# Second attention of a four-layer kernel: index scores placed inside the first query group, eight projection steps ahead of the first scores, output weights' low parts allowed from the second keys on

## What is computed

```python
a_q, a_k, a_v, b_q, b_k, b_v, i_q, i_k, i_w = jnp.split(h @ w_in, EVEN_SPLITS, axis=-1)
...
o_a = diff_attention(a_q, a_k, a_v, lam, subln, lambda_init)
...
rel = jax.nn.relu(jnp.einsum('bqhd,bkd->bqhk', qiblk.astype(jnp.float32), kif))
score = jnp.einsum('bqhk,bqh->bqk', rel, wiblk.astype(jnp.float32))
score = jnp.where(mask[None], score, -jnp.inf)
_, idx = lax.top_k(score, topk)
...
return jnp.concatenate([o_a, o_b], axis=-1) @ w_out
```

## Time and profile before

| | |
|---|---|
| median of three executions | 1785.41 us |
| the profiled execution's own time | 1787.7 us |
| span of its trace | 1785.9 us |
| mean granted TensorE clock in it | 0.987 of full |
| busy: PE, DVE, ACT | 97%, 64%, 50% |
| the stretch around the change | 960 to 1090 us of the span |

### The profile page before, as it was taken

How to read it: one execution, slowest core, us unless ns; L and a number is a source line. 1 busy time by engine, 2 the same in 40 slices (tenths; PEclk the granted TensorE clock), 3 DMA queues, 4 the chain that set the end, 5 groups by cost and what they waited for, 6 DMA issues and landing times.

```text
span 1785.9 us, 22395 instructions
## 1 busy us (share of the span) xinstructions
PE 1735.7 (97%) x9104; PEld 1444.5 (81%) x9104; DVE 1141.9 (64%) x1588; ACT 897.9 (50%) x1282; POOL 7.7 (0%) x21
## 2 busy tenths in 40 slices
PE   8999999999999999999999989999999999999998
PEld 5898788888867888888888867888888889778887
DVE  3779978779666754565547967554655556675553
ACT  4645644465657444554444566444544445574432
POOL 0000000000000000000000000000000000000000
PEclk9999999999989999999999999999999999999999
DMA  9957677866615665555555324545554556345451
GB/s 385 379 227 295 238 306 294 305 244 230 258 72 189 235 222 179 200 191 181 176 201 183 119 71 177 183 171 188 204 186 175 192 205 224 111 149 181 170 195 47
DMA packets 54984, 363.45 MB, mean 204 GB/s; under 512 B 5841, under 2 KB 9041, under 8 KB 14690
## 3 DMA queue, kind: packets, MB, share of 16 engines
q1 hardware_dynamic: 53122, 351.47, 53.6%
q0 software_dynamic: 1760, 10.56, 1.5%
HBM read 360.96 MB, written 1.05 MB: 203 GB/s over the span
## 4 chain that ended last, share of the span: by engine, by line
PE 79%; DVE 10%; ACT 2%; issue 1%; DMA 0%; DVEq 0%; ACTq 0%
PE pp L633 76%; DVE low L1892 3%; PE pp L908 2%; DVE raw L1905 1%; PE pp L840 1%; DVE hf L2036 1%; PE pp L985 1%; ACT wh L1350 1%; DVE hl L1892 0%; DVE Sb L2187 0%; DVE sc L2288 0%; DVE x L1895 0%; DVE tb L1892 0%; DVE h L1892 0%; DVE top L2285 0%
## 5 line engine op out<-in xcount | busy, mean ns | idle before, releaser
L1892 DVE TENSOR_TENSOR low<-raw,wh 128x2048 fp32r<-128x2048 f32 (+3 forms) x346 | 638.8, 1861 | 367.9 <-ACT wh L1350 367.7
L1350 ACT ACTIVATE wh<-raw 128x2048 fp32r<-128x2048 f32 (+3 forms) x352 | 537.2, 1544 | 417.5 <-PE pp L633 288.1
L633 PE MATMUL pp<-wh,hh 128*128 128x512 f32 x1312 | 522.7, 398 | 7.4 <-ACT hh L1617 2.2
L633 PE MATMUL pp<-low,hh 128*128 128x512 f32 x1312 | 514.0, 392 | 1.8 <-DVE low L1892 1.6
L633 PE MATMUL pp<-wh,hl 128*128 128x512 f32 x1312 | 507.2, 392 | 3.7 <-DVE hl L1892 3.7
L633 PEld LDWEIGHTS pp<-wh,hh 128*128 128x128 f32 x1312 | 247.6, 189 | 65.3 <-issue 13.9
L633 PEld LDWEIGHTS pp<-wh,hl 128*128 128x128 f32 x1312 | 247.5, 189 | 57.6 <-DVE hl L1892 5.0
L633 PEld LDWEIGHTS pp<-low,hh 128*128 128x128 f32 x1312 | 248.0, 189 | 51.8 <-DVE low L1892 3.5
L633 PE MATMUL pp<-wh,hidh 128*128 128x512 f32 x592 | 232.0, 392 | 0.0
L633 PE MATMUL pp<-low,hidh 128*128 128x512 f32 x592 | 230.6, 389 | 0.3 <-DVE low L1892 0.3
L633 PE MATMUL pp<-wh,hidl 128*128 128x512 f32 x592 | 230.6, 389 | 0.0
(11 more groups left out here) (226 smaller groups left out, 1190.7 us busy)
## 6 DMA issues: line engine op xcount, KB each, us to landing
raw<-in_w SPq DMA_DIRECT2D x300, 1024.0 KB, 4.8
raw<-in_w SPq DMA_DIRECT2D x24, 768.0 KB, 4.3
raw<-in_w SPq DMA_DIRECT2D x13, 512.0 KB, 19.1
firstw<-in_w SPq DMA_DIRECT2D x6, 1024.0 KB, 14.8
gain<-in_w POOLq DMA_DIRECT2D x6, 512.0 KB, 4.8
bT<-in_rel POOLq DMA_DIRECT2D x1, 2048.0 KB, 12.0
cst<-in_csts POOLq DMA_DIRECT2D x1, 1029.0 KB, 7.2
xT<-in_xT SPq DMA_DIRECT2D x1, 1024.0 KB, 5.8
```

What stands on the lines that cost most here:

```text
L633: return e.matmul(out, lhsT, rhs, start=start, stop=stop, skip_group_check=True)
L1350: q.then_inc(e.activation(wh[j % NW][:, c], raw_of(i, kt * n)[:, c], ACT.Copy), s_wh, (j, part))
L1892: return e.tensor_tensor(out, a, b, op)
```

## The change

Three things are moved, all in the first layer of the second block.

1. The first block of index scores goes into the first query group, after six of its eight steps; the second block comes behind the group, and each later block stands one place earlier against the steps of `aqk` 1. On ACT the copy of `aqk` 0 for its rotation goes behind the relus of heads 0 to 3. DVE's order in this part stays as it is.
2. Eight fill steps in place of four run ahead of the attention pipeline, on all three engines, and `even_rate` gives two steps for six iterations in place of eight. The steps of attention a's norm (`oa_sums`, `oa_square`, `oa_root`, `oa_scale`) go two fill steps further down.
3. On DVE the limit that holds back the low parts of the output weights is lifted when the keys of b are done ("b"), no longer after b's values ("bv").

```diff
         def even_rate(i):
-            return 2 if i < 8 else 1
+            return 2 if i < 6 else 1
...
-                    if n == 2:
+                    if n == 4:
                         oa_sums(0)
...
-            whole("aqk", 0, h(7), (s_sq, (("rope", "aqk", 0),)), between=idx_rest)
-            q.wait_ge(s_side, ("rope", "idx", 0))
...
+            steps = group("aqk", 0, h(7), (s_sq, (("rope", "aqk", 0),)), between=idx_rest)
+            for _ in range(6):
+                next(steps)
             for n in range(2):
                 ixp.bufs[n], ixp.ends[n] = pairs.begin(("ix", n), (s_sideact, ("rl", 0, 5 + 2 * n)))
+            q.wait_ge(s_side, ("rope", "idx", 0))
+            index_scores(1, 0)
+            run(steps)
             steps = group("aqk", 1, h(7), (s_sq, (("rope", "aqk", 1),)))
-            for qb, jj, n in ((1, 0, 2), (1, 1, 2), (0, 0, 2), (0, 1, 2)):
+            for qb, jj in ((1, 1), (0, 0), (0, 1)):
                 index_scores(qb, jj)
-                for _ in range(n):
+                for _ in range(2):
                     next(steps)
-                if (qb, jj) == (1, 0):
+                if (qb, jj) == (1, 1):
                     rope(("rope", "aqk", 0), "64", 4, misc)
...
-            for n in range(4):
+            for n in range(8):
                 fill.step()
...
             ahead.group("aqk", 0)
-            rope_copy("aqk", 0, (s_side, ("rope", "aqk", 0)))
...
+                    if (qb, j) == (1, 4):
+                        rope_copy("aqk", 0, (s_side, ("rope", "aqk", 0)))
...
                 yield "b"
+                ahead.limit = of_group[("even_out", 0)][-1] + 1
...
-                ahead.limit = of_group[("even_out", 0)][-1] + 1
                 yield "bv"
```

More of the change, by code:

```diff
@@ L1690, in even_fill @@
                 for n, _ in enumerate(ahead.steps("bv", 0, "N")):
-                    if n == 1:
+                    if n == 2:
                         oa_square(0)
-                    if n == 2:
+                    if n == 4:
                         oa_root(0)
@@ L1860, in scalar_program @@
             fill = Fill(even_fill())
-            for _ in range(4):
+            for _ in range(8):
                 fill.step()
@@ L2327, in even_fill @@
                 yield "b"
+                ahead.limit = of_group[("even_out", 0)][-1] + 1
                 tb.begin(("oa",), (s_side, ("oa", 1)))
                 for n, _ in enumerate(ahead.steps("bv", 0, "N")):
-                    if n == 3:
+                    if n == 5:
                         oa_scale(0)
                     yield
-                ahead.limit = of_group[("even_out", 0)][-1] + 1
                 yield "bv"
```

## The result

| | before | after |
|---|---|---|
| median of 11 executions | 1783.67 us | 1787.34 us |
| ratio, 95% interval | | 1.0018 (1.001 to 1.0026) |
| profiled execution | 1787.7 us | 1785.48 us |
| its span, mean granted clock | 1785.9 us, 0.987 | 1783.7 us, 0.992 |

The change costs 0.1 to 0.26%, some 3.7 us by the medians. The interval lies above 1, so it is a loss, but a smaller one than the 0.3% that the prediction took to be the least that a measurement can tell. The forecast was +4.9 us. Its 1790.3 us stood on the median of three executions, 1785.41; with eleven that median is 1783.67, so the differences are to be compared and not the times.

The account below looks back on a forecast made before the run. Bound by PE, then DVE (992 to 1037 us), then PE; +3.9 index part, +2.8 turning behind `bk`, -1.4 work done earlier, -0.4 low parts give +4.9 on 1785.4, so 1790.3 us; range 1781 to 1796.

Parts of the forecast that it names:

- Part 1: Index scores: PE stalls 2.7 us at the third block behind the rotation, and its query group ends 3.9 us late.
- the two ways past the fourth block: PE reaches the fourth index block at full clock and waits 1.5 us, or at half clock without waiting; both give 990.2.
- Part 2: Eight steps ahead: first scores at 1010.1, `bk` done 3.9 us later at 1040.9, attention b's scores 6.7 us later.
- the clock: PE's half clock around attention b's first scores costs the same 1.6 us as before, so 0; without it, -1.6.
- the 1.4 of work done earlier: PE does six matmuls of 512 columns ahead of attention b, formerly behind it: -1.4 us afterwards.
- The limit: Output weights' low parts leave the values stage, so PE's 0.4 us wait for a low part goes: -0.4 us.
- absorbed: Rival: PE's stall at the index scores doesn't reach DVE, which limits up to 1037 us; about 1785.7 us; chance 0.2.
- Faster: Rival: DVE is spared before `bk`, so PE's waits and half clocks there go; -7 us, 1778.5; chance 0.12.
- Worse: Rival: low parts behind `bk` delay DVE's chain to the turnings, adding small waits; some +8 us, 1793.4; chance 0.18.

Follow-up runs that it names:

- experiment 5: The whole change with six relu buffers of 256 columns in place of three of 512, same memory: 1781.55 against 1783.27 us before, ratio 0.9994.
- experiment 1: Only the move of the index scores and ACT's copy, four fill steps and old limit kept: 1788.95 against 1784.95 us before, ratio 1.0022.
- experiment 2: Only the eight steps ahead and the earlier limit, index scores as before: 1782.81 against 1784.95 us before, ratio 0.9989.
- experiment 6: Only the eight steps ahead, limit and index scores as before: 1781.88 against 1783.27 us before, ratio 0.9997.
- experiment 7: Eight steps, earlier limit, old index scores, plus four quarter low parts between eighth step and first scores: 1781.6 against 1783.27 us before, ratio 0.9992.
- experiment 8: The whole change with six relu buffers and four quarter low parts ahead of the scores: 1779.52 against 1783.27 us before, ratio 0.9977.
- experiment 3: The whole change with DVE's rotation of the first queries behind the additions of heads 4 to 7: 1783.69 against 1784.95 us before, ratio 0.9998.

## Why the prediction was right

Each step, all times counted from the start of the stretch, in us:

| step | before | after | moved | forecast |
|---|---|---|---|---|
| last operation of `aqk` 0's rotation, DVE | 14.81 | 15.63 | +0.82 | +0.8 |
| PE's stall at the third block | none | 2.43 | +2.43 | +2.7 |
| first scores, PE | 33.03 | 42.48 | +9.45 | +9.8 |
| idle of DVE ahead of the first reduction | none | 2.83 | +2.83 | about +3 |
| start of the last operation of `bk` | 68.51 | 72.99 | +4.48 | +3.9 |
| first scores of attention b | 69.80 | 77.02 | +7.22 | +6.7 |
| from there to the first product with `bv` | 20.27 | 17.31 | -2.96 | -1.4 |
| from that to the end | 19.47 | 18.65 | -0.82 | -0.4 |
| sum of the last three | | | +3.44 | +4.9 |

**Part 1** held in every step, and it rested on one chain read across three engines: matmul, relu, buffer, addition, rotation. Experiment 5 takes one link out of the chain and the loss is gone. Experiment 1 shows that the two ways past the fourth block give the same time. The sizes were a little high: PE's first scores are 9.45 us later and not 9.8, and DVE starts 0.52 us behind them, where I had taken 0.7. **Part 2** held too. The work taken out of DVE's run was 5.2 us: from the first reduction at 1006.19 to the end of `bk` at 1037.32 it is 31.1 us, of which 1.0 is the idle at the half clock, so 30.1 us of work, the figure that I had. And PE's turning waits for the normalising behind `bk`, 2.2 us behind it, the work of which I had put at 2.15.

**The step that failed is the clock**: "Now PE stalls 2 to 3 us ahead of 1043.1, so I take the same loss: 0." PE's waits come in two pieces, 3.15 us ahead of the rotation of `bk` and only 1.23 us ahead of attention b, since PE has turnings and six matmuls of 512 columns between them. The half clock came behind the first piece. There it costs DVE's idle of 1.0 us. Less the 0.5 us by which the first reduction came earlier than forecast, that makes `bk` +4.5 and not +3.9, and the scores +7.2 and not +6.7 (from `bk` to the scores I had +2.8, and it was +2.74). Behind the scores the loss of 1.6 us is gone: the -2.96 are the 1.4 of work done earlier and 1.56 more. So the clock gave 0.6 us net (1.6 back, 1.0 taken), not 0. How it fell is in part luck: around the same wait of 3.15 us the half clock lasted from 1028.7 to 1035.5 in after, but only from 1028.0 to 1031.4 in experiment 2. The three misses (0.5 too little at the scores, 1.6 of clock and 0.4 of the limit too much) leave the sum 1.5 us too high. **The limit** was worth 0.8, not 0.4. The wait of 0.39 us understates it: as experiment 6 shows, the matmul that waits is 0.56 us late, the next one 0.67.

The Trainium skill (TensorE: Matmul & The Clock Gate, section Loop structure matters more than you think) pictures the fall for waits of 8 us. The runs keep speaking against a reading by which waits of 2 to 3 us are harmless, though not simply so, as the last section shows.

Of the rivals, **absorbed** falls by experiment 1. **Faster** asked for the first scores no later than DVE is free; they came 2.8 us later. But its mechanism is there in weak form in experiment 2, -1.2 us in the stretch and a ratio whose interval ends at 0.9997. Low parts put in DVE's gap, in experiment 7, gave 1.5 us more in the stretch. The Trainium skill (Perfetto Trace Analysis, section Optimization Strategy) says that interleaving regimes may improve performance. Experiments 2 and 7 agree, with small gains; the whole change, which moves work in the same sense, lost. **Worse** falls: small waits did come up (0.83 for `low`, 0.69 for `st`), but ahead of the keys, where DVE sets the pace; behind attention b's first scores, where this rival put them, the time fell by 3.8 us.

## What to carry to other kernels

Before moving a step on one engine, follow its operands *and its banks* back: here a matmul waited for a relu, the relu for a buffer, the buffer for an addition, and the addition for a rotation that no one had connected with index scores. A ring of three that was large enough in the old order made +3.4 us in the new one, and a ring of six in the same memory took 4.6 us off by the first reduction. Where an engine idles after a move, put work in the gap that it does later on its crowded stretch, and size it to the gap.

## What the runs showed of the hardware

That equal waits need not have equal clocks was new to me. Behind the stall at the third block the granted clock in after and in experiment 1 was, columns as in the earlier trace rows (after first):

```profile
981.70:983.40 1.70, 1.70 (x9) 1.70 (x9) 1.20 (x2) 1.45 (x4) 0.00 (x0) 0.50 0.00 0
```

```profile
982.40:984.40 2.00, 2.00 (x18) 1.88 (x19) 1.36 (x3) 2.00 (x4) 0.00 (x0) 1.00 0.03 8
```

The waits were 2.43 and 2.44 us, and PE's instructions ahead of them the same. Behind a wait of 1.64 us in experiment 8 PE was at half clock, and behind one of 1.65 at the same place in experiment 5 at full clock (its row at 1027.22 above). The window of experiment 8:

```profile
1022.60:1024.10 1.50, 1.50 (x8) 1.05 (x8) 1.43 (x7) 1.50 (x6) 0.00 (x0) 0.50 0.63 262
```

The shortest wait with a half clock behind it was 0.83 us (experiment 5, its window at 1015.3 above); behind the same wait, of 0.83 or 0.84 us, after and experiments 2, 3 and 6 stayed at full clock. The longest with no half clock behind it was 2.44 us. Nor does the fall always come at once: behind the wait of 2.86 us in experiment 1 the granted clock was 1.00 from 1037.7 to 1038.7 and 0.55 in the us behind that. A wait's length alone doesn't decide. The cost is in where it falls: 1.6 us where PE sets the pace, 1.0 us where DVE waits for a few matmuls, and nothing where PE would have had to wait for the next buffer anyway. In experiment 5 it even helped: 1.5 us lost while PE had time to spare made the next wait as much shorter.
